# Rotated keys turned by DMA through DRAM, a slot ahead of use, in place of four TensorE transposes and a ScalarE copy

## The reference, cut to what matters

```python
def _retention(q, k, v, S0):          # chunks of c = 128 positions
    def body(S, blk):
        qc, kc, vc = blk
        sc = einsum('bihd,bjhd->bhij', qc, kc) * decay           # scores in the chunk
        o = einsum('bhij,bjhv->bihv', sc, vc) + einsum('bihd,bhdv->bihv', qc, S) * q_dec
        S = S * s_dec + einsum('bjhd,bjhv->bhdv', kc * k_dec, vc)
        return S, o
...
q = _rope(q, pos);  k = _rope(k, pos) * (RET_DK ** -0.5)          # 8 heads of 128
o, S = _retention(q, k, v, S0)
o = o * rsqrt(mean(o * o) + EPS) * silu(g_r)
vn = layernorm(v_g);  m = u * spatial_gate(vn) * silu(g_g)        # gMLP heads
h = h + concat([o, m]) @ w_out
```

## Time and profile before

| | us |
|---|---|
| median of 3 runs (lowest, highest) | 1147.77 (1146.61, 1150.92) |
| the profiled execution, its time | 1150.53 |
| its span (core 7; all cores 1139.2 to 1148.7) | 1148.7 |
| TensorE busy in the span | 1117.0 (97%) |
| VectorE, GpSimd, ScalarE busy | 789.0, 671.1, 635.7 |
| slot loop of layer 0, first slot's start to last slot's start | 133.5 to 464.9 |
| slot loop of layer 1 | 691.3 to 1022.2 |
| granted clock of TensorE, per core | 0.998 to 0.999 |

### The profile page before, as it was taken

How to read it: one execution, slowest core, us unless ns; L and a number is a source line. 1 busy time by engine, 2 the same in 40 slices (tenths; PEclk the granted TensorE clock), 3 DMA queues, 4 the chain that set the end, 5 groups by cost and what they waited for, 6 DMA issues and landing times.

```text
span 1148.7 us, 26973 instructions; the slowest of 8 cores (1139.2 to 1148.7 us)
## 1 busy us (share of the span) xinstructions
PE 1117.0 (97%) x8910; PEld 677.4 (59%) x8910; DVE 789.0 (69%) x1654; ACT 635.7 (55%) x1150; POOL 671.1 (58%) x704
## 2 busy tenths in 40 slices
PE   4999999999999999999989999999999999998997
PEld 2544566677667667545544446667667667664453
DVE  3775867777777777784574486777776777777854
ACT  3764856556556556524444487555555655662433
POOL 3267556667666666513476784666766766662332
PEclk9999999999999999999999999999999999999999
DMA  9831646546536555779680227346545546576553
GB/s 192 208 106 42 87 111 131 127 69 137 122 73 136 118 104 146 154 225 231 176 190 6 60 32 159 95 82 131 116 85 126 118 87 131 133 102 150 202 178 145
DMA packets 149720, 144.29 MB, mean 126 GB/s; under 512 B 46288, under 2 KB 119760, under 8 KB 149328
## 3 DMA queue, kind: packets, MB, share of 16 engines
q1 hardware_dynamic: 128320, 99.83, 31.2%
q0 software_dynamic: 21120, 42.48, 23.9%
q10 hardware_dynamic: 144, 0.26, 0.1%
HBM read 127.14 MB, written 44.24 MB: 149 GB/s over the span
## 4 chain that ended last, share of the span: by engine, by line
PE 90%; DMA 6%; issue 1%; DVE 1%; ACT 1%; POOL 1%; SPq 0%; DVEq 0%; ACTq 0%; POOLq 0%
PE ps L848 27%; PE ps L869 17%; PE ps L726 13%; PE ps L1292 13%; PE ps L657 4%; DMA cats<-catn 2%; PE ps L1228 2%; PE ps L949 1%; PE ps L1076 1%; PE ps L967 1%; PE ps L994 1%; PE ps L932 1%; DMA h<-hb_51 1%; PE ps L1034 1%; PE ps L997 1%
## 5 line engine op out<-in xcount | busy, mean ns | idle before, releaser
L848 PE MATMUL ps<-xnT,RW 128*128 128x512 bf16 x1536 | 359.6, 379 | 0.0
L848 PEld LDWEIGHTS ps<-xnT,RW 128*128 128x128 bf16 x1536 | 143.3, 98 | 141.4
L869 PE MATMUL ps<-RW,xnT 128*128 128x256 bf16 x1920 | 219.3, 272 | 0.0
L869 PEld LDWEIGHTS ps<-RW,xnT 128*128 128x128 bf16 x1920 | 184.1, 98 | 21.0
L897 POOL TENSOR_TENSOR kn<-A_k,B_k 128x512 bf16<-128x512 f32 x64 | 81.5, 1273 | 90.6 <-DVE B_k L893 52.8
L491 ACT ACT_TABLE_LOAD x73 | 93.7, 1283 | 44.7 <-DVE rs L1005 35.7
L491 ACT ACTIVATE B_q<-ps 64x512 f32<-64x512 f32 x128 | 75.8, 592 | 42.4 <-DVE A_q L906 36.7
L885 DVE SCALAR_TENSOR_TENSOR A_k<-ps,small,kr 128x256 f32<-128x256 f32 x128 | 56.1, 479 | 62.7 <-PE ps L869 52.5
L1015 POOL TENSOR_TENSOR catn<-og,rs 128x512 bf16<-128x512 f32 x64 | 66.0, 1045 | 41.6 <-ACT rs L491 31.1
L976 DVE SCALAR_TENSOR_TENSOR S_72<-S_72,ps 128x128 f32<-128x128 f32 x240 | 68.2, 284 | 17.4 <-DVE S_72 L976 2.9
L491 ACT ACTIVATE sgr_78<-ps 128x512 bf16<-128x512 f32 x32 | 19.1, 597 | 90.8 <-DVE B_k L893 87.1
(11 more groups left out here) (566 smaller groups left out, 2564.6 us busy)
## 6 DMA issues: line engine op xcount, KB each, us to landing
RW<-w_h POOLq DMA_DIRECT2D x80, 256.0 KB, 5.3
stt_124<-st SPq DMA_DIRECT2D x16, 512.0 KB, 5.2
stt_123<-st SPq DMA_DIRECT2D x16, 512.0 KB, 7.0
ss_out<-stt_123 SPq DMA_DIRECT2D x16, 512.0 KB, 4.1
ss_out<-stt_124 SPq DMA_DIRECT2D x16, 512.0 KB, 5.0
cats<-catn SPq DMA_DIRECT2D x28, 256.0 KB, 2.1
hb_49<-xp SPq DMA_DIRECT2D x6, 512.0 KB, 5.3
hb_50<-xp SPq DMA_DIRECT2D x6, 512.0 KB, 5.6
```

Source lines behind the costliest of these rows:

```text
L848: r = e.matmul(ps[:, b, :], w[:, k, :], xnT[:, k, s], start=(k == 0), stop=(k == 7))
L869: r = e.matmul(out(c).rearrange("p (g d) -> p g d", g=2), x, RW[:, 8 * sk + k:8 * sk + k + 9:8, :], start=(k == 0), stop=(k == 7))
```

## The change

The keys go another way to kT. After GpSimd has added kn, SyncE writes it to a new DRAM buffer kd (one 128 KB place for each slot). A new call, K_turn, loads it back through the DMA's transposed load into kT. The last slot of each layer keeps the transposes and the copy (KT). The k32 piece becomes a call of its own, K32.

In the slot the calls are in a new order: SC(p) stands behind P_gg instead of behind P_kgr, K_turn(u) right behind SC(p) (both use the one kT), and OO(p) behind P_u and K32 instead of behind P_gg. kT's contents for unit u are so asked for in slot n and used in slot n + 1, behind P_gg.

```diff
+    kd = nc.dram_tensor("kd", [H * NQ, 128, 512], BF16, kind="Internal").ap()
...
             pool(lambda e: e.tensor_tensor(out=kn[:], in0=a3, in1=b3, op=ALU.add), A_k.k() + B_k.k(), kn.k(), 512)
+            if u.n < H * NQ - 1:
+                dma("sp", kd[u.n], kn[:].rearrange("p c d -> p (c d)"), kn.k(), [("kd", u.n)], kn.name, 131072)
...
+        def K_turn(l, u):
+            dma_t(kT[:].rearrange("p (c i) -> p c i", c=4), kd[u.n], [("kd", u.n)], kT.k(), kT.name, 131072)
+
         def KT(l, u):
...
             act(kT[:], pb[:, 0:512], AF.Copy, [], kT.k() + [bk(b)], 512)
-            if u.q == 0:
-                b2 = brot()
...
+        def K32(l, u):
+            b2 = brot()
+            pe(lambda e: e.matmul(ps[:, b2, 0:32], ra2[:], identf[:, 0:32], start=True, stop=True), ra2.k() + identf.k(), [bk(b2)], 0.09)
+            dve(lambda e: e.tensor_copy(k32[:], ps[:, b2, 0:32]), [], k32.k() + [bk(b2)], 32)
...
                 P_kgr(l, u)
-                if p:
-                    SC(l, p)
                 P_q(l, u)
...
                 P_gg(l, u)
                 if p:
-                    OO(l, p, pp)
+                    SC(l, p)
+                if n < H * NQ - 1:
+                    K_turn(l, u)
                 if u.q == 3:
                     next(kv)
-                for f in (KT, P_u) if p else (P_u, KT):
-                    f(l, u)
+                P_u(l, u)
+                if n == H * NQ - 1:
+                    KT(l, u)
+                if u.q == 0:
+                    K32(l, u)
+                if p:
+                    OO(l, p, pp)
```

More of the change, by code:

```diff
@@ L935, in KT @@
             act(kT[:], pb[:, 0:512], AF.Copy, [], kT.k() + [bk(b)], 512)
-            if u.q == 0:
-                b2 = brot()
-                pe(lambda e: e.matmul(ps[:, b2, 0:32], ra2[:], identf[:, 0:32], start=True, stop=True), ra2.k() + identf.k(), [bk(b2)], 0.09)
-                dve(lambda e: e.tensor_copy(k32[:], ps[:, b2, 0:32]), [], k32.k() + [bk(b2)], 32)
+        def K32(l, u):
+            b2 = brot()
+            pe(lambda e: e.matmul(ps[:, b2, 0:32], ra2[:], identf[:, 0:32], start=True, stop=True), ra2.k() + identf.k(), [bk(b2)], 0.09)
+            dve(lambda e: e.tensor_copy(k32[:], ps[:, b2, 0:32]), [], k32.k() + [bk(b2)], 32)
         def SC(l, u):
```

## The result

The changed kernel takes 1184.74 us (median of four runs, 1172.59 to 1189.56) against 1148.14 us for the kernel before on the same chip. The ratio is 1.0296, 95% interval 1.0227 to 1.0364: 3% slower, where 1136 us had been forecast (the ratio counts a fifth run, of 1180.42). In this and all that follows, ratios and intervals leave out runs in which the cores of a die had a lower granted clock than the others or the time lay far above the rest, while medians count every run. The profiled execution, at 1172.6 us (span 1171.0), is the quickest of the four, so its trace shows somewhat less of the loss than the median has.

A forecast was written before the change was run, and what follows sets the result against it. TensorE, busy 97% of the span, was taken to bound the kernel. The profiled 1150.5 - 13.8 + 1 + 1 = 1138.7 us became, for the median, 1147.8 - 11.8 = 1136 us, range 1131 to 1147.

The forecast's parts named there:

- What bounds the kernel: Whole kernel and both slot loops: TensorE, busy 97% of the span, sets the time; a loop lasts the sum of its matmuls.
- the 13.8 us of transposes: Key transposes leaving TensorE in the slot loops: 62 groups of four at 0.223 us each come off.
- ScalarE's copy: Copy of kT from PSUM leaving ScalarE, 62 of 64 at 0.60 us, 37 us: costed at nothing, no gain either.
- SC and OO move: New call order in the slot: OO may start 1.95 us after SC, masked scores take 1.77 us, so nothing.
- Two DMAs per slot: Key write and transposed load on SyncE's queue: at most 6.0 us from kn to kT on quiet rings, no wait.
- 5 us to spare: Ordinary slots: keys land by 318.3, the next slot's scores are due at about 323.3, so no wait.
- Once per head it is tight: Change from q = 3 to q = 0, 14 places: keys 0 to 0.4 us late, 0 to 5.6 us, taken as 1 us.
- The queue that the new DMAs share: SyncE's in-order issue: transfers behind the waiting turned load come 2 to 3 us later, covered by distance; costed at nothing.
- The end of layer 1: Last slots of layer 1, where output weights crowd the rings: late keys cost 0 to 18 us, taken as 1 us.
- Late keys once per head: Rival at the change of heads: turned load lands behind stt_124's load, 3.3 us x 14 = 46 us, 1180 us; chance 0.10.
- OO waits for scT: Rival in slots with state updates: masked scores come too late for the output matmul, 22 us, 1156 us; chance 0.07.
- the gain doesn't arrive: Rival in the slot loops: freed TensorE time becomes idle because another engine sets slot length, 1145 to 1150 us; chance 0.08.

## Why the prediction was wrong

*What bounds the kernel, and the 13.8 us of transposes:* right. Without waits for keys in them the loops are 324.7 and 323.8 us, and 29 groups at 0.223 us each off make 324.9 and 324.4.

*ScalarE's copy at nothing:* right; ScalarE is 19.6 and 19.4 us less busy per loop than in the earlier trace rows, and the time didn't follow it.

*SC and OO move, at nothing:* right for the changed kernel. No wait of OO for scT stands in its list. It is what returns when SC is set later still. The working has one slip, which moves nothing: before, SC stood 315.08 - 310.59 = 4.5 us ahead of OO, not 3.9.

*Two DMAs per slot, "5 us to spare", and "Once per head it is tight ... I take 1 us in all":* this is the step that failed. The mechanism was named, keys that land behind the states' transfers, but the term was mis-sized: where it has 1 us for fourteen places, the seven waits there are 17.4 us on the profiled core, and two slots that were to have 5 us to spare waited 2.5 and 3.1 us. It was wrong in three ways. First, the landing. I had kT 6.0 us behind kn on quiet rings and at most 10.1 us at the change of heads. The whole run's medians are

```profile
kd<-kn SPq DMA_DIRECT2D x62, 128.0 KB, 2.1
...
kT<-kd SPq DMA_TRANSPOSE x62, 4.7
VV<-cats SPq DMA_TRANSPOSE x36, 5.4
```

so a turned load of 128 KB takes 4.7 us, more than the 3.9 that the earlier trace rows gave for 256 KB and that I took as an upper end, and that row itself rose to 5.4 with the new traffic. At the change of heads the load was issued 7.2 us behind the keys' write in the slot shown, since SyncE was held by other issues; I had read SyncE's plain issues, 0.4 to 0.5 us, and none of a turned one, though the trace of the kernel before has one of 1.49 us at 301.56 us, between the two state transfers. Second, the spare time belonged to one slot: the run that spared the fourth unit found the first unit's keys late by up to 3.6 us, and the run that moved its turn ahead found its own keys still late, by 2.0 us in the slot shown. Third, no term stood for the clock. I priced a wait at its length, and the wait of 4.1 us was followed by at least 3.6 us of work at granted clock 0.50. Why the keys are late is shown in part only: the states' transfers carry about 24 of the 37 us, neither cats' turned load ahead nor the single buffer explains the rest by itself, and that rest is open.

*The queue that the new DMAs share, at nothing:* wrong in part, for the same reason. SyncE's issue is in the chain with 4%.

*The end of layer 1, 1 us:* in the changed kernel little shows there on the profiled core, so about right; the earlier trace rows was the right warning, and it came true in the kernels without state transfers and with only two units, at the end of either loop.

*The rivals.* "Late keys once per head" gave 1180 and is the nearest in time, and the late keys are there. Its mechanism holds only in part: the turn stood ahead of stt_124's load, not behind it, only seven of fourteen places waited over 1 us, and about 24 of the 37 us go when the states' transfers go. The 6.6 us of stt_123's load, named there as agreeing, stood behind a 512 KB store, ss_out<-stt_124, issued 0.5 us before it at 304.47 us, and not behind another load. "OO waits for scT" and "the gain doesn't arrive" did not happen.

## What to carry to other kernels

When a transfer replaces work on the bounding engine, price the arrival of its data by the transfers of the stage that it will share the DMA engines with, not by quiet rows, and ask whether its reader can wait: here a saving of 13.8 us was lost to nine waits of 1 to 4 us on the profiled core, five of which were paid again in clock. A kernel with the transfers in place and the waits taken away, on the data already there, tells in one run what the change could give (1137 us) and so whether there is something to repair. Moving the late reader back moves the wait to the next engine; leaving the tight units on the old path, with a small margin for the rest, gave 3 us.

## What the runs showed of the hardware

- The turned load of 128 KB is cut small. DMA packets rose from 149720 to 192376, those under 512 B from 46288 to 81008: 34720 / 62 = 560 small packets per unit. In a stretch with no other transfer on SyncE's queue but the turned load (352.8 to 357 us) it moved 544 packets, all of them under 512 B. The Trainium skill (Advanced Engine Details and Errata, X-Bar Transpose (TRN2)) has such transfers as fast as regular ones. No run here decides it: the turned load took 4.7 us where the plain write of the same 128 KB took 2.1, but plain loads of 64 and 256 KB (gmb_161 and RW) took 5.0 and 6.0 by median.
- In the changed kernel the issue of a turned load held SyncE for 1.2 to 4.0 us, most plain ones for 0.3 to 0.6.
- Behind waits of 2.0, 2.1, 3.1, 3.8 and 4.1 us in the changed kernel TensorE worked at granted clock 0.50, the 1.2 GHz level, for some 3 to 5 us, fully busy; behind two waits of 2.5 us it stayed at 1.00. The length of a wait alone did not tell whether the clock fell.
- While a 512 KB load on GpSimd's queue moved, a turned load on SyncE's nearly stopped: 92 packets against 20 in the 2 us from 380 us (state loads on GpSimd's queue).
